# Opening transfers reordered, first key weights by quarters, and three steps of the second block moved forward

## The reference

```python
# block 1 (x, and a context of 256 tokens that only feeds the recurrent state)
sh1, sc1, gt1, sh2, sc2, gt2 = split(silu(c) @ w_ada + b_ada, 6)      # and the same with c_ctx
h  = rmsnorm(x, g_mix) * (1 + sc1) + sh1                              # and for ctx
q, k, v, g, dd, cb, cc, ch, ga, gb = split(h @ w_in)                  # dd: 32 columns, decay rank
o  = bidirectional gated linear attention(q, k, v, decays(dd @ w_dec_up))
x  = x + gt1 * (merge(o, g, conv(cc * ch) * cb, ga, gb) @ w_mix_out)
x  = x + gt2 * swiglu(modulated norm(x)); x = rmsnorm(x, g_final)
# block 2
x  = x + 0.5 * g1 * swiglu(...)
z  = h @ w_in_2                       # q_lat, kv_lat, k_pe, ca_q, ca_k, ca_v, gate_a, gate_b
ya = mla_attention(..., rope(positions)) @ w_branch_a
yb = chunk_attention(..., rel_bias) @ w_branch_b
x  = x + g2 * ((sigmoid(gate_a) * ya + sigmoid(gate_b) * yb) @ w_out)
x  = x + 0.5 * g3 * swiglu(...); out = rmsnorm(x, final_norm)
```

## Time and profile before

| | |
|---|---|
| median of 3 runs | 1139.32 us |
| profiled execution, time | 1138.17 us |
| profiled execution, span | 1136.4 us |
| mean granted clock of TensorE | 0.992 |
| PE busy | 1099.3 us, 97% |
| DVE busy | 820.3 us, 72% |
| ACT busy | 571.8 us, 50% |
| POOL busy | 73.0 us, 6% |

### The profile page before, as it was taken

How to read it: one execution, slowest core, us unless ns; L and a number is a source line. 1 busy time by engine, 2 the same in 40 slices (tenths; PEclk the granted TensorE clock), 3 DMA queues, 4 the chain that set the end, 5 groups by cost and what they waited for, 6 DMA issues and landing times.

```text
span 1136.4 us, 18424 instructions
## 1 busy us (share of the span) xinstructions
PE 1099.3 (97%) x7660; PEld 991.4 (87%) x7660; DVE 820.3 (72%) x924; ACT 571.8 (50%) x733; POOL 73.0 (6%) x143
## 2 busy tenths in 40 slices
PE   2999999999999999999999999999999999999997
PEld 2899989999999888888788888889999997888885
DVE  1578695886677777777888877888777777655555
ACT  2495453544434554444653544456655546444453
POOL 4000000100000000000300000011000001000001
PEclk8999999999999999999999999999999999999999
DMA  9934556788856587877578788748965654655550
GB/s 282 312 111 146 188 167 199 234 279 259 292 196 209 187 296 244 294 258 256 185 261 297 251 266 276 240 158 252 287 192 184 222 181 132 220 186 186 191 195 37
DMA packets 180258, 250.25 MB, mean 220 GB/s; under 512 B 4859, under 2 KB 147390, under 8 KB 180062
## 3 DMA queue, kind: packets, MB, share of 16 engines
q1 hardware_dynamic: 171550, 216.92, 58.2%
q0 software_dynamic: 8640, 32.38, 8.5%
HBM read 248.23 MB, written 1.05 MB: 219 GB/s over the span
## 4 chain that ended last, share of the span: by engine, by line
PE 86%; DVE 6%; ACT 3%; issue 2%; SPq 2%; DMA 1%; POOL 0%; POOLq 0%; DVEq 0%; ACTq 0%
PE twin L1287 84%; DVE wlo L1911 2%; DVE arena L1919 2%; ACT whi L864 1%; ACT arena L864 1%; DMA arena<-in_w_ada 1%; DVE arena L1911 1%; DVE X L1911 1%; PE twin L1627 1%; SPq L515 1%; SPq L561 0%; DVE arena L1915 0%; ACT A_both L864 0%; PE twin L1747 0%; PE twin L1421 0%
## 5 line engine op out<-in xcount | busy, mean ns | idle before, releaser
L1287 PE MATMUL twin<-A_both,whi 128*128 128x256 f32 (+1 forms) x2208 | 577.8, 339 | 1.5 <-DVE A_both L1911 1.0
L1911 DVE TENSOR_TENSOR wlo<-raw,whi 128x2048 fp32r<-128x2048 f32 (+1 forms) x171 | 386.9, 2264 | 137.7 <-ACT whi L864 137.2
L1287 PE MATMUL twin<-A_both,wlo 128*128 128x256 f32 x1632 | 436.6, 280 | 0.0
L864 ACT ACTIVATE whi<-raw 128x2048 fp32r<-128x2048 f32 x169 | 323.1, 1912 | 175.6 <-PE twin L1287 174.2
L1287 PEld LDWEIGHTS twin<-A_both,whi 128*128 128x128 f32 x2208 | 370.2, 190 | 45.0 <-issue 7.1
L1287 PEld LDWEIGHTS twin<-A_both,wlo 128*128 128x128 f32 x1632 | 309.3, 190 | 11.4 <-DVE A_both L1911 0.6
L1919 DVE SCALAR_TENSOR_TENSOR arena<-ada_raw,arena 128x512 f32<-128x512 f32 x182 | 137.3, 755 | 22.2 <-DMA ada_raw<-in_w_ada 3.9
L864 ACT ACTIVATE arena<-twin 128x512 f32<-128x512 f32 (+5 forms) x171 | 90.8, 556 | 122.5 <-PE twin L1287 91.9
L864 ACT ACTIVATE arena<-arena 128x512 f32<-128x512 f32 (+7 forms) x132 | 69.6, 558 | 159.8 <-DVE arena L1911 126.7
L1287 PE MATMUL twin<-whi,B_hi 128*128 128x512 f32 (+2 forms) x340 | 125.4, 369 | 0.3 <-DVE B_lo L1911 0.3
L1287 PE MATMUL twin<-wlo,B_hi 128*128 128x512 f32 (+2 forms) x340 | 125.1, 368 | 0.0
(11 more groups left out here) (137 smaller groups left out, 861.0 us busy)
## 6 DMA issues: line engine op xcount, KB each, us to landing
raw<-in_w_in SPq DMA_DIRECT2D x48, 1024.0 KB, 6.7
raw<-in_ffn_w_in SPq DMA_DIRECT2D x44, 1024.0 KB, 5.1
ada_raw<-in_w_ada POOLq DMA_DIRECT2D x28, 1024.0 KB, 5.7
ada_raw<-in_w_ada SPq DMA_DIRECT2D x24, 1024.0 KB, 5.1
raw<-in_w_ffn_in SPq DMA_DIRECT2D x22, 1024.0 KB, 5.1
raw<-in_ffn_w_out SPq DMA_DIRECT2D x22, 1024.0 KB, 5.1
raw<-in_w_ffn_out SPq DMA_DIRECT2D x11, 1024.0 KB, 5.5
arena<-in_w_ada SPq DMA_DIRECT2D x8, 1024.0 KB, 12.0
```

The costliest lines, as they stand in the source:

```text
L864: return nc.scalar.activation(o, i, f, **kw)
L1287: return nc.tensor.matmul(o, l, r, start=start, stop=stop, **kw)
L1911: return nc.vector.tensor_tensor(o, x, y, op)
```

## The change

It touches three places.

1. **Transfers.** SP issues ctx and x first, then the vectors, then per quarter q: `ada0[q]`, `ada0[4+q]`, and behind the next quarter's pair the weights of the quarter, `load_quarter(q)`: 32 KB of `dd` (2 of 8 k-blocks, now 32 columns) and 256 KB of the first `k` unit. Each pair has a semaphore of its own, `start_w[q]`. ACT and DVE split `k` by quarters (`start_split(q)`, 128x512). POOL issues `g_head` and `wdec` after its norms and after `start_cols` 3 (PE's `turn_rows(2)`).
2. **Order on the engines in the opening.** PE turns ctx and x first, then the vectors, then `start_modulation(0)`, `turn_rows(0)`, and ten extra matmuls on `ones` (`keep_warm(0, 10)`). ACT takes `squares` before it copies the vectors. DVE takes its norms before `start_copy(0)`.
3. **Block 2.** The angles are computed on DVE inside `ffn(1)`, step 0, between its first and second sum; the Sins on ACT at the end of `ffn(1)`; the `inv` memsets on POOL before the turned copies. `out_group(1, ...)`, `merge_high(1, ...)` and `merge_low(1, ...)` stand one product earlier, behind bra 0.

```diff
-        dd_w = ada_flat[:, 768:768 + KD * P].rearrange("p (k w) -> p k w", k=KD)
+        dd_w = ada_flat[:, 768:768 + KD * 2 * RANK].rearrange("p (k w) -> p k w", k=KD)
...
-            load_start(0)
-            load_start(4)
+            def load_quarter(q):
+                ks = slice(2 * q, 2 * q + 2)
+                sp.dma_start(dd_w[:, ks, :], unit_source("dd", 0)[0][:, ks, :]).then_inc(start_w[q], 16)
+                sp.dma_start(raw[1][:, 2 * UC * q:2 * UC * q + 2 * UC].rearrange("p (k w) -> p k w", k=2),
+                             unit_source("k", 0)[0][:, ks, :]).then_inc(start_w[q], 16)
             sp.dma_start(ctxX, a["ctx"].rearrange(tok, p=P)).then_inc(x_in[0], 16)
+            sp.dma_start(X[:], a["x"].rearrange(tok, p=P)).then_inc(x_in[1], 16)
...
-            sp.dma_start(X[:], a["x"].rearrange(tok, p=P)).then_inc(x_in[1], 16)
-            load_unit(0, *P1[0])
-            load_unit(1, *P1[1])
-            for j in (1, 5, 2, 6, 3, 7):
-                load_start(j)
+            for q in range(4):
+                load_start(q)
+                load_start(4 + q)
+                if q:
+                    load_quarter(q - 1)
+            load_quarter(3)
...
+            norm(0)
+            norm(1)
+            pool.wait_ge(start_cols, 3)
             pool.dma_start(ghb, a["g_head"][0].partition_broadcast(P)).then_inc(gh_in, 16)
             for i in range(4):
...
-            norm(0)
-            norm(1)
...
+            def start_split(q):
+
+                cs = slice(2 * UC * q, 2 * UC * q + 2 * UC)
+                act.wait_ge(start_w[q], 32)
+                ins = run(whi[1][:, cs], raw[1][:, cs])
...
             start_quarter(0)
-            split(1, count=2)
+            start_split(0)
             start_quarter(1)
+            start_split(1)
             start_quarter(2)
+            start_split(2)
+            start_split(3)
             start_quarter(3)
             split(2)
...
                 split(u0 + 3 * NF)
+                if f == 1:
+                    rotations()
...
-                    if (kind, n) == ("bra", 1):
+                    if (kind, n) == ("bra", 0):
                         out_group(1, 0)
                         out_group(1, 1)
...
             turn_rows(0)
-            start_turn(0, 0, 1)
-            start_turn(1, 0, 1)
+            keep_warm(0, 10)
             start_modulation(1)
...
                     tt(pair3(sF), pair3(aF), twin[b // 2][:, :, 0:T], ALU.add).then_inc(first_sum, 1)
+                    if (f, i) == (1, 0):
+                        angles()
```

More of the change, by code:

```diff
@@ L316, in build @@
         start_ada = [sem(f"start_ada{j}") for j in range(8)]
+        start_w = [sem(f"start_w{q}") for q in range(4)]
+        start_hi = sem("start_hi")
+        start_lo = sem("start_lo")
         c_in = sem("c_in")
@@ L831, in _ @@
             gate_bias(2)
+            for f in range(HR):
+                ins = nc.gpsimd.memset(inv[:, f:f + 1], float(10000.0 ** (-2.0 * f / ROPE)))
+            ins.then_inc(inv_done, 1)
             pool.wait_ge(u_in, 16)
@@ L864, in run, with split @@
                 return nc.scalar.activation(o, i, f, **kw)
-            def split(u, i=0, count=1):
+            def split(u, i=0):
                 if isinstance(i, int) and u + 3 * i >= UNITS:
@@ L872, in split @@
                     act.wait_ge(unit_used, lin(3, i, u - RING + 1))
-                run(whi[ring(u)][:], raw[ring(u)][:]).then_inc(hi_ready, count)
+                run(whi[ring(u)][:], raw[ring(u)][:]).then_inc(hi_ready, 1)
             def squares(n):
@@ L1217, in second, with rotations @@
                         run(v, v, ACT.Sigmoid).then_inc(gates_done, 1)
-                    if P2[n2] == ("bra", 1):
-                        merge_high(1, 0)
-                        merge_high(1, 1)
                 partial_squares(5)
                 evac2(N2 - 1)
+            def rotations():
+                act.wait_ge(ang_done, 1)
+                f2 = "p t r -> p (t r)"
+                run(sin.rearrange(f2), ang, ACT.Sin)
+                run(cos.rearrange(f2), nrd, ACT.Sin).then_inc(trig_done, 1)
             def merge_high(kk, m):
@@ L1236, in _ @@
             run(c3.rearrange("p k s -> p s k"), craw, ACT.Silu).then_inc(c_silu, 1)
+            squares(0)
+            squares(1)
             act.wait_ge(vec_tr, 1)
@@ L1810, in key_part @@
             def key_part(q):
+                if q < 3:
+                    pe.wait_ge(start_lo, q + 1)
+                else:
+                    pe.wait_ge(lo_ready, 2)
                 if q == 0:
-                    pe.wait_ge(lo_ready, 2)
                     pe.wait_ge(vec_done, 1)
@@ L1929, in split @@
                 dve.wait_ge(hi_ready, lin(3, i, u + 1))
-                rest(wlo[ring(u)][:], raw[ring(u)][:], whi[ring(u)][:]).then_inc(lo_ready, count)
+                rest(wlo[ring(u)][:], raw[ring(u)][:], whi[ring(u)][:]).then_inc(lo_ready, 1)
             def split_part(u, part):
@@ L2017, in start_quarter, with start_split @@
                     rest(lo[:, ks, :], start_h[s][q], hi[:, ks, :]).then_inc(hlo_done, 2)
+            def start_split(q):
+                cs = slice(2 * UC * q, 2 * UC * q + 2 * UC)
+                if q < 3:
+                    dve.wait_ge(start_hi, q + 1)
+                else:
+                    dve.wait_ge(hi_ready, 2)
+                ins = rest(wlo[1][:, cs], raw[1][:, cs], whi[1][:, cs])
+                if q < 3:
+                    ins.then_inc(start_lo, 1)
+                else:
+                    ins.then_inc(lo_ready, 2)
             def affine(n, k):
@@ L2369, in output_rows, with angles @@
                         ALU.mult).then_inc(out_done, 1)
[L2371 to L2375 removed]
+            def angles():
                 dve.wait_ge(pos_in, 16)
@@ L2392, in second, with bias_col @@
                 ts(nrd, nrd, -1.0, math.pi / 2, ALU.mult, ALU.add).then_inc(ang_done, 1)
+            def bias_col(n):
+                blk, c0 = ADA[NORM_UNITS[n][0]]
+                return (0 if blk == 0 else 48) + c0 // P
+            def second():
                 gate_row(3)
@@ L2504, in second @@
                         evac2(n2 - 1)
+                    if P2[n2] == ("bra", 1):
+                        merge_low(1, 0)
+                        merge_low(1, 1)
                     if P2[n2 - 1] == ("brb", 1):
@@ L2540, in second @@
                 evac2(N2 - 1)
-            start_copy(0)
             norm(0)
             norm(1)
+            start_copy(0)
             start_quarter(0)
-            split(1, count=2)
+            start_split(0)
             start_quarter(1)
+            start_split(1)
             start_quarter(2)
+            start_split(2)
+            start_split(3)
             start_quarter(3)
```

41 lines of the change are left out of this document (17 added, 24 removed).

## The result

The changed kernel takes 1130.72 us (median of 4 runs, 1129.46 to 1131.03); the kernel before, measured beside it, 1138.98 us (1138.55 to 1139.71). The ratio is 0.9926, 95% interval 0.9912 to 0.9940: **8.3 us faster**, where 5.3 us were forecast. The profiled execution took 1129.46 us, its span is 1127.7 us.

A forecast was written before the change was run, and what follows sets the result against it. PE is busy 97% of the span; transfers bound the opening up to 30.7 us and nearly so after. Opening 3.8, angles 0.44 and turned heads 1.07 sum to 5.3 us gained: median 1134.0 us, range 1131.5 to 1137.3 us.

The forecast's parts named there:

- the new wait: Opening: `turn_rows(3)` waits for DVE's quarter 3 copy, queued behind splits 2 and 3; 43.6 us in place of 42.3.
- 0.44 and 1.07 us of waits: Block 2: moving the angles removes a 0.44 us weight-split wait; turning heads behind bra 0 removes 1.07 us for `B_lo`.
- short packets: Opening's `dd` loads: 128-byte packets cost only their bytes, 0.09 us a quarter; if slow, 0.75 us a quarter.
- rival 3: Next stage, 60 to 100 us, or late units 3 and 4 eat the opening's gain; 1137.8 us, chance 0.07.
- rival 5: Opening: PE's clock stays low and a quarter takes about 13 us; slower, 1144 us, chance 0.05.
- The third and fourth: Opening: by bytes, third modulation's data at 32.0 us, fourth's at 38.9, plus 1.1 for POOL's loads: fourth starts at 40.0.
- The forecast of 3.8: Gain of the opening in us: `turn_rows(3)` at 43.6 us, where it came at 47.4 before.
- The matmuls on `ones`: Opening, ahead of the second modulation: ten take 1.1 us of a wait, priced at nothing.
- Everything else PE loses lies ahead of 30.8 us: Whole kernel: after 55 us the change can touch only PE waits of 1.07 and 0.44 us; other losses come earlier.
- Rival 1: Opening: quarter splits do not hold up the copy, the fourth modulation's start sets all; 6.6 us gained, 1132.7 us, chance 0.16.

The follow-up runs named there:

- pool_late_only: Kernel before, with only POOL's `g_head` and eight w_dec_up loads moved behind its norms and PE's third turned row; 1136.77 us, ratio 0.9979 to before.
- angles_back: Changed kernel with the angles, Sins and `inv` memsets put back to the start of block 2's attention; 1131.60 us, ratio 0.9930 to before.
- wide_dd: Changed kernel with `dd` loaded 128 columns wide again (0.52 MB in place of 0.13); 1134.08 us, ratio 0.9949 to before.
- wdec_early: Changed kernel with POOL's `g_head` and w_dec_up loads issued ahead of its norms again; 1133.02 us, ratio 0.9945 to before.
- block2_only: Kernel before with only the three moves in block 2 (angles and Sins, `inv` memsets, turned heads); 1136.92 us, ratio 0.9983 to before.
- small_on_sp: Kernel before with `g_head` and the eight w_dec_up loads issued by SP ahead of x, in place of POOL; 1138.79 us, ratio 0.9995 to before.
- wdec_late_only: Kernel before with only the eight w_dec_up loads moved behind POOL's norms and PE's third turned row, `g_head` left in front; 1137.84 us, ratio 0.9987.

## Why the prediction was right or wrong

**Right:** the direction; that transfers bound the opening, with PE's own pace close behind; the mechanism of the new wait (0.83 us, forecast 1.3), its place, and that it ends on `wlo`; 0.44 and 1.07 us of waits gone in block 2, the moves costing nothing elsewhere; short packets as cheap as their bytes; nothing eaten at 60 to 100 us (rival 3); the clock at 1.00 from the second modulation on (rival 5).

**The step that failed** is "The third and fourth": w_ada for the fourth modulation at 40.0 us, and with it the last quarter of `k` at 41.7. It landed at 37.35 us, and PE started that modulation at its own pace at 37.57 us; the quarter of `k` came at 39.1. The last two pieces of w_ada in the changed kernel, issued at 25.56 and 26.75 us, answer to the earlier trace rows:

```profile
L564 SPq DMA_DIRECT2D arena<-in_w_ada x2: 1146/1778/2411, 25.6 to 26.8; - x2
...
DMA to landing us min/median/max: 8.8/9.7/10.6
```

The first of the two took 8.8 us and landed at 34.4 us; the last took 10.6 us, which gives 37.35 us. Of the 2.65 us between 40.0 and 37.35:

- 1.4 us were there at the second modulation already. Its data came at 23.7 us (issued 11.7, 12.0 to landing), not 25.1, 7.0 us sooner than before. POOL's loads were priced by their bytes at 1.1 us; `pool_late_only` measures 2.67 us. The other 1.57 MB, priced at 4.5 us, make the remaining 4.3.
- 1.1 us were added for POOL's loads in the last quarter. They are issued from 34.19 us on, but up to 37.35 us the trace has no packet of theirs; all 304 run between then and 45 us. They fell behind this piece.
- The last 0.15 us are within the rounding: from 23.7 to 37.35 us are 13.65 us, where the forecast had 38.9 - 25.1 = 13.8. So counting on by bytes from an earlier landing was right, and so were the 1.7 us from the last w_ada to the last quarter of `k`.

Both wrong terms are prices of the same 0.39 MB: too low for the place that it left, too high for the one to which it went. Why it cost more than its bytes in the first place is open, as said above.

With PE's rows alone the opening reads: second modulation 6.0 us sooner (7.0 by data, 1.1 back for the matmuls on `ones`), 1.4 us more for a first quarter at full clock (7.83 to 6.39), 0.8 back for the copy, 6.5 in all. The forecast of 3.8 was 2.7 short.

**Two smaller misses.** The matmuls on `ones` took 2.79 us, not 1.1 (the 56 ns of the estimate are of a 128*32 matmul, these are 128*128), and did stand on the path; that cost nothing only because the copy sets the end. And the two waits of block 2 paid 0.7 and 1.3 us, 0.5 us more than their idle time. 2.7 + 0.5 us is the error of 3.3 us, within what a median can tell. "Everything else PE loses lies ahead of 30.8 us" is not so: from 60 us on the kernel before also has six waits of PE for DVE's `arena` with 3.3 us in all and four for `A_both` with 1.2, which the change does not touch. **Rival 1** (the splits do not hold the copy, 1132.7 us) was right in its two conditions, that the small transfers land closely behind w_ada and that POOL's share comes late, but wrong in its mechanism: the splits held the copy, and PE waited 0.83 us for it. Its time was nearer all the same, and the low end of the range rested on it.

## What to carry to other kernels

Where transfers bound a stretch, count on by bytes from a landing of before: over 13.7 us that was right within 0.2. But price small loads by their share of the DMA engines' time, not by their MB: POOL's nine made 1.1 us by bytes, 2.0 us by the share, and 2.67 us in the run. And do not charge a load to a piece because the two are issued near each other: look at when its packets run. Then lay PE's own pace beside the transfers and see which of the two ends last. And when a wait on one engine is taken out of a stretch that transfers bound, look for the next piece in the queue: here two such moves, and an earlier issue, gave nothing.

## What the runs showed of the hardware

- One row read for 128 partitions (0.13 MB) took 1.15 us of all 16 DMA engines in one profile, three times its bytes, and 1.7 us on the path by the marks of two profiles.
- POOL's loads, issued from 34.19 us on while SP's transfers kept the engines busy, had no packet on the engines before 37.35 us.
- The last pieces of a queue can land late in one execution and not in another: the last w_ada at 38.5 us in the profile of `angles_back`, at 37.35 and 37.1 us in the two of the changed kernel. The low rates behind such pieces (86 GB/s from 42 to 44 us there, 173 from 44 to 47 us in `wide_dd`, 138 in `wdec_early`) begin while SP waits for DVE's split before it issues more, and end some 2 us after it has issued.
- A wait of PE of 1.07 us was worth 1.3 to 1.4 us, one of 0.44 us 0.7 us.
- In the order of before, PE's quarter behind the pause took 7.83 us in the profile shown, and 8.67, 8.68 and 8.51 us in those of `block2_only`, `small_on_sp` and `wdec_late_only`: the granted clock rose at a different time. The changed opening, with 6.4 us each time from the second modulation on in both its profiles, is also free of that.
